# Three attentions of a Trainium2 kernel: scores one block further ahead, and the softmax division moved into the matrix product that turns the probabilities

## The reference

```python
scores = jnp.einsum('bcqhd,bckhd->bhcqk', qc, kb).astype(jnp.float32) * (Dh ** -0.5)
scores = scores + bias[None, :, None, :, :]
scores = jnp.where(valid[None, None, :, None, :], scores, jnp.float32(-1e30))
probs = jax.nn.softmax(scores, axis=-1).astype(v.dtype)
out = jnp.einsum('bhcqk,bckhd->bcqhd', probs, vb)        # probabilities times values
```

## Time and profile before

| | us |
|---|---|
| median of 3 runs | 3627.7 |
| the profiled execution | 3628.0 |
| its span | 3626.3 |
| PE busy | 3476.9 (96%) |
| DVE busy | 1734.7 (48%) |
| ACT busy | 797.5 (22%) |

### The profile page before, as it was taken

One profiled execution on the slowest core, in us unless ns is written; L12 is line 12 of the kernel. 1 busy time (PEld: TensorE's weight loads), 2 busy tenths in 40 slices (PEclk: granted clock), 3 DMA queues, 4 the chain that ended last, 5 costly groups with the idle time before them and its releaser, 6 DMA issues.

```text
span 3626.3 us, 42139 instructions
## 1 busy us (share of the span) xinstructions
PE 3476.9 (96%) x17032; PEld 2779.7 (77%) x17032; DVE 1734.7 (48%) x2080; ACT 797.5 (22%) x1170; POOL 1201.5 (33%) x534
## 2 busy tenths in 40 slices
PE   7999999989999999989999999999999999999997
PEld 5767877778888888777876678888888877777675
DVE  4323433352323323588866642332322368888835
ACT  4433100020000000332234430000000141343452
POOL 2222344323433433233321033343343414332222
PEclk9999999999999999999999999999999999999998
DMA  2111211111111111122111011111111101111111
GB/s 95 39 36 38 93 47 46 47 34 47 46 52 46 46 52 46 35 66 82 59 34 33 23 41 52 47 46 51 47 46 58 47 18 59 59 59 56 46 35 64
DMA packets 52164, 178.98 MB, mean 49 GB/s; under 512 B 5728, under 2 KB 6368, under 8 KB 52064
## 3 DMA queue, kind: packets, MB, share of 16 engines
q1 hardware_dynamic: 38016, 138.43, 11.7%
q10 hardware_dynamic: 14048, 39.10, 3.2%
HBM read 172.79 MB, written 4.72 MB: 49 GB/s over the span
## 4 chain that ended last, share of the span: by engine, by line
PE 85%; DVE 8%; ACT 3%; issue 3%; POOL 1%; DMA 0%; ACTq 0%; DVEq 0%; POOLq 0%
PE acc L390 70%; PE acc L408 4%; PE acc L751 2%; PE acc L727 2%; PE acc L427 2%; PE acc L716 2%; DVE rstd L614 1%; PE acc L474 1%; DVE normed L660 1%; DVE conv_slots L1740 1%; DVE x_lo L489 0%; PE acc L499 0%; DVE h L904 0%; POOL w_lo L2067 0%; DVE window_scores L784 0%
## 5 line engine op out<-in xcount | busy, mean ns | idle before, releaser
L2053 POOL TENSOR_TENSOR w_hi<-raw,zero 128x1024 fp32r<-128x1024 f32 x264 | 516.8, 1958 | 2368.5 <-PE acc L390 1662.8
L390 PE MATMUL acc<-x_hi,w_hi 128*128 128x512 f32 x2512 | 778.4, 391 | 5.7 <-POOL w_lo L2067 3.1
L390 PE MATMUL acc<-x_lo,w_hi 128*128 128x512 f32 x2512 | 774.3, 389 | 0.0
L390 PE MATMUL acc<-x_hi,w_lo 128*128 128x512 f32 x2512 | 774.0, 389 | 0.0
L2067 POOL TENSOR_TENSOR w_lo<-raw,w_hi 128x1024 fp32r<-128x1024 f32 x262 | 678.3, 2589 | 20.5
L904 DVE TENSOR_TENSOR h<-h,acc 128x1024 f32<-128x1024 f32 x312 | 380.7, 1221 | 555.1 <-PE acc L390 555.0
L390 PEld LDWEIGHTS acc<-x_hi,w_hi 128*128 128x128 f32 x2512 | 470.0, 188 | 106.7 <-POOL w_lo L2067 4.8
L390 PEld LDWEIGHTS acc<-x_lo,w_hi 128*128 128x128 f32 x2512 | 472.0, 188 | 98.7
L390 PEld LDWEIGHTS acc<-x_hi,w_lo 128*128 128x128 f32 x2512 | 471.8, 188 | 98.5
L1171 DVE TENSOR_TENSOR hid<-act_g,acc 128x1024 f32<-128x1024 f32 x44 | 53.7, 1221 | 570.8 <-PE acc L390 554.7
L484 ACT ACTIVATE hid_hi<-hid 128x1024 fp32r<-128x1024 f32 x44 | 46.7, 1061 | 909.2 <-DVE hid L1171 909.2
(11 more groups left out here) (335 smaller groups left out, 4053.8 us busy)
## 6 DMA issues: line engine op xcount, KB each, us to landing
raw<-blocks SPq DMA_DIRECT2D x264, 512.0 KB, 3.4
near_bias<-bias ACTq DMA_DIRECT2D x16, 512.0 KB, 4.0
h<-x_t ACTq DMA_DIRECT2D x8, 512.0 KB, 8.7
h<-x_t ACTq DMA_DIRECT2D x1, 4096.0 KB, 15.3
q_past<-q_dram ACTq DMA_DIRECT2D x8, 512.0 KB, 5.4
w_own<-r_dram ACTq DMA_DIRECT2D x8, 512.0 KB, 6.5
out_t<-out_rows ACTq DMA_DIRECT2D x8, 512.0 KB, 3.0
band_bias<-bias ACTq DMA_DIRECT2D x4, 640.0 KB, 3.9
```

Source lines behind the costliest of these rows:

```text
L390: ins = pe.matmul(acc[s][:, c], w[:, slot, tile, :], part[:, c], start=(n == 0 and m == 0), stop=(n == last and m == 2))
L2053: pool.tensor_tensor(hi, whole, nothing, ALU.add).then_inc(hi_split, 1)
```

## The change

- `norm_probs` no longer multiplies the probabilities. It takes both heads' reciprocals in one instruction, and for each head multiplies the 128 x 128 identity by the column of reciprocals (a diagonal tile, `inverse`).
- `turn_probs` no longer is `pe.transpose` against the identity, but a plain fp32 `pe.matmul` of the unnormed probabilities with the diagonal tile, which turns and divides at once. This is in all three attentions.
- In the first and third attention PE computes the scores one block ahead, DVE runs `take_scores(p)` ahead of `norm_probs(p - 1)`, and row sums are kept twice (`own`). The second had this order already. The `memset` of `small` is done once for a pair of heads and not once a block.
- The third attention gets a buffer of its own for the scores. As this and the first one's have room for one block, `take_scores(p)` now waits for the exponential of block p - 1.
- The first attention's loop is written out, four times the same.

```diff
 def att_tensor(pe, t, a, keys, next_block=True, joint=False):
-            ahead = 1 if joint else 0
+            sink = 1 if joint else 0
...
                 def turn(bank, side, c, at):
                     w = min(P, count - c * P)
-                    return pe.transpose(turned[bank][0:w, at * P:(at + 1) * P],
-                                        a.probs[:, p % 2, side, ahead + c * P:ahead + c * P + w], ident[:, :])
+                    return pe.matmul(turned[bank][0:w, at * P:(at + 1) * P],
+                                     a.probs[:, p % 2, side, sink + c * P:sink + c * P + w],
+                                     a.inverse[:, p % 2, side, :], start=True, stop=True)
...
-            for n in range(ahead):
-                score(n)
+            score(0)
             for n in range(TT + 2):
-                if n + ahead < TT:
-                    score(n + ahead)
+                if n + 1 < TT:
+                    score(n + 1)
...
             # second attention (window_vector_steps)
             def norm_probs(p):
-                count, own = keys(p)[1], 8 * (p % 2)
+                own = 8 * (p % 2)
                 for side in range(2):
                     dve.wait_ge(exp_done, t.next("exp_done"))
-                    ch.link(dve.reciprocal(small[:, own + 4 + side:own + 5 + side],
-                                           small[:, own + 2 + side:own + 3 + side]))
-                    ch.sync()
-                    probs = a.probs[:, p % 2, side, 1:1 + count]
-                    dve.tensor_scalar(probs, probs, small[:, own + 4 + side:own + 5 + side], None, ALU.mult)\
-                       .then_inc(p_ready, 1)
+                ch.link(dve.reciprocal(small[:, own + 4:own + 6], small[:, own + 2:own + 4]))
+                ch.sync()
+                for side in range(2):
+                    dve.tensor_scalar(a.inverse[:, p % 2, side, :], ident[:, :], small[:, own + 4 + side:own + 5 + side],
+                                      None, ALU.mult).then_inc(p_ready, 1)
...
             # first and third attention (att_vector)
                 slots = [await_acc(dve, t) for _ in range(2)]
-                ch.link(dve.memset(small[:, 60:61], 3e38))
-                ch.sync()
                 for side, s in enumerate(slots):
+                    if p:
+                        dve.wait_ge(exp_done, t.next("exp_done"))
                     dve.tensor_tensor_reduce(
-                        out=a.probs[:, p % 2, side, 0:count] if a.scores is None else a.scores[:, side, 0:count],
+                        out=a.scores[:, side, 0:count], in0=acc[s][:, 0:count], in1=table[:, side, :], scale=-1.0,
...
+            ch.link(dve.memset(small[:, 60:61], 3e38))
+            ch.sync()
             for p in range(TT + 1):
+                if p < TT:
+                    take_scores(p)
                 if p >= 1:
                     norm_probs(p - 1)
-                if p < TT:
-                    take_scores(p)
...
         def att1_tensor(pe, t):
             feature_pair(pe, t, expect_parts(t, KT))
-            with t.loop(2, acc0=20, acc1=20, block=6, p_ready=32, turned_copied=40, hi_ready=2, lo_ready=2):
-                for _ in range(2):
+            for _ in range(HEAD_PAIRS):
```

More of the change, by code:

```diff
@@ L35, with __init__ @@
 class Buffers:
-    def __init__(self, q_t, k_t, v_tok, v_t, scores, probs, probs_t, total, bias):
-        self.q_t, self.k_t, self.v_tok, self.v_t, self.scores = q_t, k_t, v_tok, v_t, scores
+    def __init__(self, q_t, k_t, v_tok, v_t, scores, probs, inverse, probs_t, total, bias):
+        self.q_t, self.k_t, self.v_tok, self.v_t, self.scores, self.inverse = q_t, k_t, v_tok, v_t, scores, inverse
         self.probs, self.probs_t, self.total, self.bias = probs, probs_t, total, bias
@@ L247, in mixer_program @@
         mix_lo = at("mix_lo", 120, [P, TOK], F32R)
-        local = attention_buffers("local_", 120, 151, 182.25, 3 * P)
+        local = attention_buffers("local_", 120, 151, 196.125, 182.25, 3 * P)
         local.q_t = at("local_queries", 124, [P, TOK])
@@ L263, in mixer_program @@
             q_t=at("near_q_t", 140.625, [P, TOK]), k_t=at("near_k_t", 144.625, [P, TOK]),
-            v_tok=at("near_v_tok", 148.625, [P, TT, P]), v_t=at("near_v_t", 156.625, [P, TOK]), scores=None,
-            probs=at("near_probs", 152.625, [P, 2, 2, 640]), probs_t=at("near_probs_t", 162.625, [P, 2, 2, 5, P]),
+            v_tok=at("near_v_tok", 148.625, [P, TT, P]), v_t=at("near_v_t", 156.625, [P, TOK]),
+            scores=at("near_scores", 176.625, [P, 2, 576]),
+            inverse=at("near_inverse", 197.625, [P, 2, 2, P]), probs=at("near_probs", 152.625, [P, 2, 2, 640]), probs_t=at("near_probs_t", 162.625, [P, 2, 2, 5, P]),
             total=at("near_att_sum", 172.625, [P, TOK]), bias=None)
@@ L826, in norm_probs @@
-            def norm_probs(p):
-                count = keys(p)[1]
-                for side in range(2):
-                    dve.wait_ge(exp_done, t.next("exp_done"))
-                    ch.link(dve.reciprocal(small[:, 4 + side:5 + side], small[:, 2 + side:3 + side]))
-                    ch.sync()
-                    probs = a.probs[:, p % 2, side, 0:count]
-                    dve.tensor_scalar(probs, probs, small[:, 4 + side:5 + side], None, ALU.mult).then_inc(p_ready, 1)
+                for side, s in enumerate(slots):
+                    if p:
+                        dve.wait_ge(exp_done, t.next("exp_done"))
+                    dve.tensor_tensor_reduce(
+                        out=a.scores[:, side, 0:count], in0=acc[s][:, 0:count], in1=table[:, side, :], scale=-1.0,
+                        scalar=small[:, 60:61], op0=ALU.add, op1=ALU.min,
+                        accum_out=small[:, own + side:own + side + 1]).then_inc(acc_free[s], 1)
@@ new lines, in norm_probs @@
+            def norm_probs(p):
+                own = 8 * (p % 2)
+                if p == TT - 1:
+                    for _ in range(2):
+                        dve.wait_ge(exp_done, t.next("exp_done"))
+                ch.link(dve.reciprocal(small[:, own + 4:own + 6], small[:, own + 2:own + 4]))
+                ch.sync()
+                for side in range(2):
+                    dve.tensor_scalar(a.inverse[:, p % 2, side, :], ident[:, :], small[:, own + 4 + side:own + 5 + side],
+                                      None, ALU.mult).then_inc(p_ready, 1)
@@ L859, in exponential @@
                 act.wait_ge(acc_free[s], t.count(f"acc{s}"))
[L860 to L863, removed]
+                own = 8 * (p % 2)
+                act.activation(a.probs[:, p % 2, side, 0:count], a.scores[:, side, 0:count], ACT.Exp,
+                               scale=-1.0, bias=small[:, own + side:own + side + 1],
+                               accum_out=small[:, own + 2 + side:own + 3 + side]).then_inc(exp_done, 1)
             def copy_turned(p):
@@ L925, in att1_tensor @@
             feature_pair(pe, t, expect_parts(t, KT))
-            with t.loop(2, acc0=20, acc1=20, block=6, p_ready=32, turned_copied=40, hi_ready=2, lo_ready=2):
-                for _ in range(2):
[L928 to L932, removed]
+            for _ in range(HEAD_PAIRS):
+                projections_tensor(pe, t)
+                att_tensor(pe, t, band, keys_1)
+                feature_block(pe, t)
+                t.next("hi_ready")
+                t.next("lo_ready")
@@ L934, in att1_scalar @@
         def att1_scalar(act, t, ch):
             ch.reset()
[L936 to L945, removed]
+            for n in range(HEAD_PAIRS):
+                act.dma_start(band.bias[:, :, :], bias_1[n]).then_inc(bias_in, 16)
+                qkv_scalar(act, t, band)
+                att_scalar(act, t, ch, band, keys_1)
+                split_hi(act, t, band.total[:, :], att_hi[:, n, :])
+                t.next("lo_ready")
@@ L947, in att1_vector @@
         def att1_vector(dve, t, ch):
             ch.reset()
[L949 to L957, removed]
+            for n in range(HEAD_PAIRS):
+                pass_acc(t, 4)
+                dve.wait_ge(bias_in, t.next("bias_in") * 16)
+                att_vector(dve, t, ch, band, keys_1)
+                split_lo(dve, t, band.total[:, :], att_hi[:, n, :], att_lo[:, n, :])
```

11 lines of the change are left out of this document (3 added, 8 removed).

## The result

| | before | changed |
|---|---|---|
| median, us | 3627.4 (4 runs, 3625.1 to 3630.4) | 3716.5 (4 runs, 3713.4 to 3720.4) |
| ratio | | 1.0245 [1.0232, 1.0257] |
| span of the profiled execution | 3626.3 | 3714.4 |
| granted clock, mean | 0.986 | 0.984 |

The kernel became 89 us slower (2.5%). I had forecast 3683 and a range of 3658 to 3708: the sign was right, the size was not. 55 us were forecast.

A forecast was written before the change was run, and what follows sets the result against it. PE, busy for 96% of the span, was taken to bound the kernel. The three attentions' 18.7 + 9.6 + 26.6 = 54.9 us on the profiled 3628.0 gave 3683 us, 1.5% slower; range 3658 to 3708 for 8 in 10.

The forecast's parts named there:

- Price of a turn: All three attentions: 0.224 us a product against 0.118 a transpose, 0.106 added, 74.6 us more PE work over 704 turns.
- What idle time absorbs: PE waits in the pairs' first blocks, and ACT's copy waits in the second attention, take part of the added turn work.
- The order: Pair starts of the first and third attention, placed by hand with new waits; these attentions were forecast at +18.7 and +26.6 us.
- Low clock: First attention: 16.4 us without it, 22 with it, 18.7 taken; a low stretch covers 1.4 us of work.
- Rival 1: Pair starts: the clock stays up; chance 0.10, mostly inside the forecast range.
- Rival 2: First blocks: all PE idle time takes turn work, so the low bounds hold, 3662 us; chance 0.08.
- Rival 3: All added PE work is paid and score-buffer waits cost 10 us in two attentions, 3713 us; chance 0.11.
- Rival 4: Turns: the product with a diagonal tile runs at a transpose's cadence, 0.118 us, giving 3613 us; chance 0.05.
- DVE's shorter work: Smaller scalings on DVE are worth nothing beside full PE work in later blocks, but shorten a wait in first blocks.
- three signs of being wrong: Ten turns under 1.6 us; PE idle in full blocks for exponentials or copies; rest of program moving over 3 us.

The follow-up runs named there:

- fill: Plain products of no use on idle PE at pair starts, first and third attention; added to the kernel before 3620.2 us, to the changed kernel 3697.3 us.
- order alone: Changed kernel with turns by transpose and the old full scaling of probabilities on DVE put back; 3648.5 us, ratio 1.0058.
- diagonal products, old order: Changed kernel with the order of before in the first and third attention, products with the diagonal tile kept; 3699.0 us, ratio 1.0189.
- reduced products: Changed kernel with the old order, probabilities and diagonal tile stored as reduced fp32, one record a turn; 3654.3 us, ratio 1.0066.

## Why the prediction was wrong, point by point

The sum had 54.9 us and 88.5 came: 33.6 were missed. Pair sums of the four kernels with and without fill, us:

| | without fill | clock held | difference |
|---|---|---|---|
| before | 397.4 | 390.1 | 7.3 |
| order alone | 418.9 | 407.9 | 11.0 |
| diagonal products, old order | 469.0 | 457.7 | 11.3 |
| changed | 485.9 | 467.0 | 18.9 |

The added time comes apart in one walk: before to before filled -7.3; diagonal products +67.6 (to 457.7); the order +9.3 (to 467.0); and the fill taken out again +18.9 (to 485.9). Sum 88.5. The order costs 9.3 here and 17.8 (407.9 - 390.1) under transposes, since products fill part of its waits; the walk's steps depend on their sequence by these 8.5 us. Low clock does not add up either: each part alone loses 4 us more to it than the kernel before, both together 11.6. Each kernel has one profiled execution, and the fill is not free: in the fourth pair of the first attention scores 2 came 3.46 us behind scores 0 with it and 3.34 without. So each step may be off by a us or two.

In the prediction's own terms the 33.6 us are: 8.5 the price of a turn; some 14 low clock (18.9 us, where the sum had 2.3 in the first attention and left the third the 2.9 that it had before); and the other 11 the placing at full clock, 4.5 of them in the second attention, where the order had not changed.

- **Price of a turn: too low by a tenth.** I put 0.224 us for a product, from the cadence within a long row of `keep_clock`, against 0.118 for a transpose with its group's seams. The one was without the seam, the other with it. Ten turns take 2.42, so 0.118 a turn is added and not 0.106: 704 x 0.118 = 83.1 us, 8.5 more than my 74.6. That was just over my upper bound of 0.116.
- **What idle time absorbs: right in two attentions, half in the second.** I let it swallow 74.6 - 54.9 = 19.7 us: 6.7, 9.1 and 3.9 in the three attentions. Products with the clock held and nothing else moved lost 83.1 - 67.6 = 15.5: 28.3 - 20.9 = 7.4, 20.8 - 16.1 = 4.7 and 34.0 - 30.4 = 3.6. In the second attention I expected ACT's waits to be filled whole. They fell from 3.1 to 2.1 us and stayed at 0.5 a pair, as these copies themselves wait for PE's values of an earlier block and move with them (my reading of the code; no run parts it).
- **The order: given no price of its own, cost 9 to 20 us.** This step failed. I placed the start of a pair, with new waits in it, and what the placing swallowed is about what products alone had swallowed: the order took another 9.3 us that the sum doesn't have. At full clock the fourth pair of the first attention was placed at 38.6 us and took 40.3 with fill; from the second scores on, the second pair of the third was placed at 41.5 and took 43.4 (3274.66 to 3318.01). The price of a turn is 0.7 and 0.9 of these misses. The waits for DVE rose from 8.0 to 10.1 us in the first attention, where I expected them near 8, and from 8.8 to 14.5 in the third. In the order alone they were 16.1 and 14.5, with 4.6 and 2.3 for late probabilities besides.
- **Low clock: the other failed step, and the largest.** I let the first attention have 2.3 us of it in all (18.7 - 16.4), and left the third as it was. By the filled kernels it was 10.1 (171.7 - 161.6) and 8.9 (194.0 - 185.1), where the kernel before had 4.4 and 2.9. My 1.4 us of work for each low stretch came from one piece of one; the stretches of before were already 3 to 7 us long. In the fourth pair now it lasts until about 305, and my placing of that pair shows it: scores 4 forecast at 8.15, came at 303.35 - 292.27 = 11.08; scores 5 at 11.3, came at 15.17. From there on I lose only the seams: 43.4 against 38.6. In the third attention scores 4 came 3.3 us late, 2.7 of it from the two rows at half clock, 3289.09 and 3291.42.
- **Rival 1, that the clock stays up at the pairs' starts, fell.** All eight pairs had a low stretch (mean granted clock 0.88 to 0.96 over a pair), where seven had before (0.90 to 0.96; I had counted six). Products in place of transposes did not shorten it: my measure of it is 17 us with transposes, 20 with products alone, and 51 with reduced products, all three in the old order.
- **Rival 2 (holes swallow more) fell:** its bounds had them swallow 40 us of 74.6; products alone lost 15.5.
- **Rival 3 had nearly the right total (3713) by luck.** More waits and more low clock did come, but at the start of each pair. Its number was made of waits for the score buffer in full blocks, and there are none: the longest wait in a full block of the first and third attention is 0.31 us, for copies, and the kernel before had it too.
- **Rival 4 fell** with the two records, 480, 352 and 576 of them, and ten turns in 2.42 us.
- **DVE's shorter work: worth nothing**, as forecast for full blocks. Products with and without it are 3699.0 and 3698.9; in the new order with transposes 3650.8 and 3648.5.

None of my three signs of being wrong came: ten turns took more than 1.6 us, PE did not stand in full blocks for more than before, and the rest moved by 0.4 us. They watched the full blocks, and the error lay in the first ones.

What stays open: why low stretches that have begun last 3 to 7 us in the kernel before, 3 to 10 in the changed one and 10 to 20 with reduced products, with PE busy for most of them; and why the two parts together lose more to the clock than each for itself.

## What to carry to other kernels

Before folding a scale into a matrix product that stands in for a transpose, count the records: on a TensorE that was busy for 96% the second record cost 0.118 us, as much as the transpose, and relief on VectorE gave nothing back. With one record and the clock held, the fold came out about even (3617.6 against 3620.2). Before moving work a block ahead, look at what covers the waits of the first blocks now; what is queued behind the earlier instruction no longer covers them (8.0 us of waits for VectorE in the first attention became 16.1 with the order alone). And after any change to a start with waits in it, read the granted clock stretch by stretch: a few products with no use in the waits were worth 8, 19 and 37 us here, and without them turns as cheap as transposes read as 26 us dearer.

## What the runs showed of the hardware beyond what I expected

- A reduced fp32 product of 128 x 128 x 128 is one record (704 for 704 turns) and follows its neighbour about as fast as a transpose. In the old order without fill ten took 1.16 us at full clock in the third attention (transposes of before there, 3242.60 to 3243.84: 1.24), and 1.27 in the first (303.96 to 305.23; transposes of before, 291.40 to 292.64: 1.24).
- Low clock outlived the waits by far: behind a wait of 1.79 us, 16.0 us at a granted 0.50 with TensorE busy in all of it (second pair of the third attention, reduced products in the old order).
- The fill held the clock without covering all waits. In the filled order-alone kernel PE still stands 1.11 and 0.76 us in the first blocks, and the granted clock is 1.00 over the whole of every pair.
- The mean granted clock of the whole run hides it: 0.984 and 0.986 for the two kernels, and 0.992 for the filled changed one, which is 19 us faster.
